# Memory attention's scores as three products of rounded halves

## The reference, cut to what matters

```python
def memory_cross_attention(h, mem_n, w_cq, w_ck, w_cv, w_co):
    q = (h @ w_cq).reshape(bsz, seqlen, 4, 256)
    k = (mem_n @ w_ck).reshape(bsz, mlen, 4, 256)
    v = (mem_n @ w_cv).reshape(bsz, mlen, 4, 256)
    logits = jnp.einsum('bqhd,bkhd->bhqk', q, k,
                        preferred_element_type=jnp.float32) * (256 ** -0.5)
    p = jax.nn.softmax(logits, axis=-1)
    o = jnp.einsum('bhqk,bkhd->bqhd', p.astype(v.dtype), v).reshape(bsz, seqlen, 1024)
    return o @ w_co
```

## Time and profile before

| what | value |
|---|---|
| median of 3 runs | 2120.2 us (2120.08 to 2120.25) |
| the profiled execution's own time | 2120.16 us |
| its span, first to last instruction | 2118.3 us |
| TensorE, matmul records, busy | 2108.1 us (100%) |
| TensorE, weight loads, busy | 1741.2 us (82%) |
| VectorE busy | 826.1 us (39%) |
| ScalarE busy | 808.3 us (38%) |
| GpSimd busy | 1120.8 us (53%) |
| granted TensorE clock | 1.000 of full speed |

### The profile page before, as it was taken

The page is one execution under the profiler, slowest core; times in us unless marked ns, Lnnn a source line. Parts: engine busy times, 40 slices in busy tenths (PEclk is TensorE's granted clock), DMA queues, the critical chain, the costliest instruction groups (busy, mean ns, idle before and its releaser), DMA issues.

```text
span 2118.3 us, 29185 instructions
## 1 busy us (share of the span) xinstructions
PE 2108.1 (100%) x10122; PEld 1741.2 (82%) x10122; DVE 826.1 (39%) x1486; ACT 808.3 (38%) x1364; POOL 1120.8 (53%) x1493
## 2 busy tenths in 40 slices
PE   9999999999999999999999999999999999999999
PEld 7888888878888778877888888887787898888898
DVE  5222211762941766143322221208753374013234
ACT  5222222325833656323322232325654353122234
POOL 6555555673344338725655555554454476555554
PEclk9999999999999999999999999999999999999999
DMA  6322333223322213412332223232222223332222
GB/s 212 122 99 99 99 100 110 85 96 102 116 89 90 73 58 123 156 40 90 99 99 93 95 99 110 100 97 73 80 80 80 90 90 105 103 100 99 99 90 80
DMA packets 61344, 207.71 MB, mean 98 GB/s; under 512 B 6616, under 2 KB 8088, under 8 KB 61256
## 3 DMA queue, kind: packets, MB, share of 16 engines
q1 hardware_dynamic: 55216, 195.84, 27.9%
q10 hardware_dynamic: 6040, 10.65, 1.6%
HBM read 204.31 MB, written 4.77 MB: 99 GB/s over the span
## 4 chain that ended last, share of the span: by engine, by line
PE 54%; issue 22%; POOL 21%; DVE 1%; ACT 1%; DMA 0%; POOLq 0%; SPq 0%; ACTq 0%; DVEq 0%
POOL w_lo L469 21%; PE bank L522 15%; PE bank L524 15%; PE bank L523 15%; PE bank L684 1%; PE bank L686 1%; PE bank L685 1%; PE bank L950 1%; PE bank L925 1%; PE bank L848 1%; PE bank L937 0%; DMA x<-xT 0%; PE bank L854 0%; PE bank L747 0%; PE bank L852 0%
## 5 line engine op out<-in xcount | busy, mean ns | idle before, releaser
L469 POOL TENSOR_TENSOR w_lo<-w_raw,w_hi 128x256 fp32r<-128x256 f32 x1448 | 1087.2, 783 | 926.7 <-ACT w_hi L1305 926.6
L522 PE MATMUL bank<-gx_hi,w_hi 128*128 128x512 f32 (+1 forms) x1768 | 674.4, 381 | 1.4 <-DVE gx_lo L2461 1.0
L524 PE MATMUL bank<-gx_hi,w_lo 128*128 128x512 f32 (+1 forms) x1768 | 668.1, 378 | 0.0
L523 PE MATMUL bank<-gx_lo,w_hi 128*128 128x512 f32 (+1 forms) x1768 | 667.6, 378 | 0.0
L1305 ACT CAST w_hi<-w_raw 128x1024 fp32r<-128x1024 f32 x364 | 378.5, 1045 | 346.1 <-PE bank L524 285.0
L522 PEld LDWEIGHTS bank<-gx_hi,w_hi 128*128 128x128 f32 x1768 | 332.7, 188 | 64.6 <-issue 2.3
L524 PEld LDWEIGHTS bank<-gx_hi,w_lo 128*128 128x128 f32 x1768 | 332.6, 188 | 62.4
L523 PEld LDWEIGHTS bank<-gx_lo,w_hi 128*128 128x128 f32 x1768 | 332.8, 188 | 60.5 <-issue 0.2
L522 PE MATMUL bank<-ff_hi,w_hi 128*128 128x512 f32 x352 | 136.9, 389 | 0.0
L523 PE MATMUL bank<-ff_lo,w_hi 128*128 128x512 f32 x352 | 136.9, 389 | 0.0
L524 PE MATMUL bank<-ff_hi,w_lo 128*128 128x512 f32 x352 | 136.9, 389 | 0.0
(11 more groups left out here) (361 smaller groups left out, 2703.5 us busy)
## 6 DMA issues: line engine op xcount, KB each, us to landing
w_raw<-wstream SPq DMA_DIRECT2D x364, 512.0 KB, 3.5
bias_spread<-bias_rows ACTq DMA_DIRECT2D x1, 2560.0 KB
square<-cum_rows ACTq DMA_DIRECT2D x8, 256.0 KB, 3.7
rfin_row<-cum_rows ACTq DMA_DIRECT2D x8, 256.0 KB, 3.2
outT<-ple_o SPq DMA_DIRECT2D x8, 256.0 KB, 2.0
x<-xT SPq DMA_DIRECT2D x3, 512.0 KB, 8.1
square<-bias_spread ACTq DMA_DIRECT2D x4, 256.0 KB, 2.6
rfin_row<-bias_spread ACTq DMA_DIRECT2D x4, 256.0 KB, 2.7
```

Of the source, the lines that this page charges most:

```text
L469: ins = nc.gpsimd.tensor_tensor(w_lo[:, s, part], w_raw[:, s, part], w_hi[:, s, part].bitcast(F32), ALU.subtract)
L522: nc.tensor.matmul(dst, hi, rhs[0], start=first, stop=False)
L523: nc.tensor.matmul(dst, hi, rhs[1], start=False, stop=False)
L524: return nc.tensor.matmul(dst, lo, rhs[0], start=False, stop=last)
```

## The change

The keys `kx_T` are rounded by ScalarE into `kx_hi` (in `round_k`, between the weight units of `cv`), and VectorE makes the rest `kx_lo`, in place of `kx_T`, when the last unit of `cv` is done. Each query chunk is rounded by ScalarE into `qx_hi` (`round_q`), and VectorE makes `qx_lo` in place of `qx_T` (`low_q`). `x_score` is then six matmuls of rounded operands instead of two in full fp32, and a head's first score waits for `score_lo`. `scale_q` moves from the end of VectorE's odd iterations to their start, and `low_q` takes its place at the end. Two semaphores of memsets are replaced by VectorE's own chain.

```diff
+        kx_hi = at("kx_hi", 16, [DC, ML], F32R)
+        kx_lo = at("kx_lo", 0, [DC, ML], F32R)
+        qx_hi = at("qx_hi", 24, [DC, S], F32R)
+        qx_lo = at("qx_lo", 48, [DC, S], F32R)
...
                 if i == 0:
-                    pe.wait_ge(tile_free, TILE0["cq"] + 2 * hd + 2)
-                for e in range(2):
-                    mm = nc.tensor.matmul(bank[2 + n % 2][:, 0:ML], qx_T[:, 2 * hd + e, i * P:(i + 1) * P],
-                                          kx_T[:, 2 * hd + e, :], start=(e == 0), stop=(e == 1))
+                    pe.wait_ge(sem("score_lo"), DC + 2 * hd + 2)
+                dst = bank[2 + n % 2][:, 0:ML]
+                for c in (2 * hd, 2 * hd + 1):
+                    qh, ql = (q[:, c, i * P:(i + 1) * P] for q in (qx_hi, qx_lo))
+                    nc.tensor.matmul(dst, qh, kx_hi[:, c, :], start=(c == 2 * hd), stop=False)
+                    nc.tensor.matmul(dst, qh, kx_lo[:, c, :], start=False, stop=False)
+                    mm = nc.tensor.matmul(dst, ql, kx_hi[:, c, :], start=False, stop=(c == 2 * hd + 1))
                 mm.then_inc(sem("x_score"), 1)
...
+            def round_k(c):
+                act.wait_ge(tile_free, TILE0["ck"] + c + 1)
+                nc.scalar.copy(kx_hi[:, c, :], kx_T[:, c, :]).then_inc(sem("score_hi"), 1)
             for g in range(2):
-                token_evac("cv", g, vx, m_rstd, MT, ACT.Copy, (sem("m_col"), 1), banks=CV_BANKS[g])
+                token_evac("cv", g, vx, m_rstd, MT, ACT.Copy, (sem("m_col"), 1), between=round_k, banks=CV_BANKS[g])
             ahead("cq", 0, 4, 0)
             norm("n_cross")
             ahead("cq", 0, 4, 1)
             ahead("cq", 0, 4, 2)
+
+            def round_q(c):
+                act.wait_ge(tile_free, TILE0["cq"] + c + 1)
+                nc.scalar.copy(qx_hi[:, c, :], qx_T[:, c, :]).then_inc(sem("score_hi"), 1)
+            round_q(0)
+            round_q(1)
             for n in range(XH * TT + 4):
+                if n % 2 == 1 and n < 12:
+                    round_q(2 + n // 2)
...
-            nc.vector.memset(conv_in[:, 0:3], 0.0).then_inc(sem("conv_pad"), 1)
-            dve.wait_ge(sem("conv_pad"), 1)
+            link(nc.vector.memset(conv_in[:, 0:3], 0.0))
...
             scaled_tiles("ck", kx_T, 8, row=m_row, banks=CK_BANKS)
+            dve.wait_ge(unit_done, UNIT0["cq"])
+            for c in range(DC):
+                dve.wait_ge(sem("score_hi"), c + 1)
+                nc.vector.tensor_tensor(kx_lo[:, c, :], kx_T[:, c, :], kx_hi[:, c, :].bitcast(F32), ALU.subtract)\
+                  .then_inc(sem("score_lo"), 1)
             norm("n_cross")
...
+            def low_q(c):
+                dve.wait_ge(sem("score_hi"), DC + c + 1)
+                nc.vector.tensor_tensor(qx_lo[:, c, :], qx_T[:, c, :], qx_hi[:, c, :].bitcast(F32), ALU.subtract)\
+                  .then_inc(sem("score_lo"), 1)
             scale_q(0)
             scale_q(1)
+            low_q(0)
+            low_q(1)
             for n in range(XH * TT + 5):
+                if n % 2 == 1 and n < 12:
+                    scale_q(2 + n // 2)
...
                 if n % 2 == 1 and n < 12:
-                    scale_q(2 + n // 2)
+                    low_q(2 + n // 2)
...
-            nc.vector.memset(cprod[:, 0:2], 0.0).then_inc(sem("cprod_pad"), 1)
+            link(nc.vector.memset(cprod[:, 0:2], 0.0))
```

## The result

| what | before | after |
|---|---|---|
| median of 11 runs each, side by side | 2120.33 us (2120.08 to 2122.21) | 2125.78 us (2124.98 to 2127.52) |
| ratio after to before | | 1.0024, interval 1.0016 to 1.0033 |
| profiled execution's span | 2118.3 us | 2124.7 us |
| granted TensorE clock | 1.000 | 0.998 |

The change costs 5.5 us, slower by more than the 0.2% that was called measurable. The forecast was 2119.5, its range 2117.5 to 2121.5: wrong in size and in sign.

A forecast was written before the change was run, and what follows sets the result against it. TensorE was taken as the bound, its matmul records covering 2108.1 of 2118.3 us. Scores -2.6, keys 0, first query chunks +1.9 and other heads 0 gave -0.7 us from 2120.16: 2119.5, range 2117.5 to 2121.5.

The forecast's parts named there:

- term 2: Key rests after `cv`: eight subtractions, 7.0 us in all, covered, so 0 us; uncovered 0 to 1 us.
- term 3: First two query chunks: rounding and subtraction delay the first score, a stall of 1.9 us (0.8 to 2.0).
- Term 1: Scores: six matmuls take 0.71 us a block instead of 0.87, gaining 2.6 us over 16 (2.2 to 3.5).
- Term 4: Other heads and the two memsets: `low_q` has 1.3 us of cover or more, so 0 us.
- D: `score_lo` late at every head: three more stalls of 1.9 us, 2125.2 us; chance 0.04.
- E: Six score matmuls bound by their weight loads, 1.13 us instead of 0.71: 6.7 us more, 2126.2; chance 0.03.
- Rival C: VectorE late for the row of `n_cross`, or GpSimd for the second `cq` tile: 0.6 to 1 us, 2120.3; chance 0.06.
- The lock: Port shared by VectorE and GpSimd: exclusive blocking would make a pair 1.14 us; the sum used the trace's 0.88.

The follow-up runs named there:

- the dead additions at 849.5 and 860.4: The kernel before plus one VectorE addition of two SBUF tiles whose result nothing reads, started at 849.49 or 860.39 us: 2124.27 and 2124.36 us.
- the copy: The kernel before plus one VectorE copy from SBUF to SBUF whose result nothing reads, when `cv` is done: 2122.50 us.
- the addition at 854.7: The kernel before plus one VectorE addition of two SBUF tiles whose result nothing reads, when unit 2 of `cv` is done: 2122.76 us.
- the memset: The changed kernel with a VectorE memset of 0.17 us in front of the first `kx_lo`: 2124.64 us.
- one dead addition's run: The kernel before plus one VectorE addition of two SBUF tiles whose result nothing reads, when `cv` is done, ahead of `n_cross`: 2120.61 us.

## Why the prediction was wrong

**The failed step is term 2, "The keys, nothing".** It priced eight subtractions at the pair's pitch of 0.88 us and wrote them off against a cover of 1.5 us. The pitch was right for a VectorE that gets its turn: with a short break in GpSimd's run the eight were over at 878.10. But here the first one got no turn for 10.7 us, and the row of `n_cross` came 4.3 us late. The rows that I took the pitch from are from a stretch in which VectorE comes every microsecond or two; the place of the change is one in which it had met GpSimd for the last time near 833 us and GpSimd had worked through 37 us since the earlier trace rows. That difference stood in the rows and went unused: `cv` has VectorE at 0.00. The profiled execution lies 7.0 us above the forecast: 4.3 are the late row, 1.6 the half clock behind it, 1.6 the second stretch, 0.3 what the scores gave less there, and term 3 takes back 0.8.

**What it hung on.** With the norm first: -5.8 us. With a pause in GpSimd: -6.7. Those are the same cure twice, for both take away the late row (4.3 us) and the clock's fall behind it (1.6); the norm first trades the first score's stall for one of 1.7 us at a bank.

**The clock, not in the prediction at all.** After a gap of 4.56 us TensorE was granted 0.50 (1.2 GHz of 2.4) for 3.4 us, worth 1.6 us over the 24 products (all gaps here are counted from start to start). After gaps at the row of 2.34 and 2.37 us it fell to 0.50 too (the dead additions at 849.5 and 860.4); after gaps of 2.19 and 2.37 (the copy, and the addition at 854.7) it stayed at 1.00, and their times are 2122.50 and 2122.76 against 2124.27 and 2124.36: the fall is worth 1.5 to 1.9 us there too. After 3.9 us behind the memset it stayed at 1.00 there and fell at 1363.5. The windows at 884 to 886 us of the additions from 849.5 and 854.7, a fence for each kernel (busy, then the granted clock):

```profile
884.00:886.00 2.00, 2.00 (x6) 0.50 0.39 154
```

```profile
884.00:886.00 2.00, 2.00 (x10) 1.00 0.44 174
```

So the gap's length alone doesn't settle the fall; what else does stays open, as does the cause of the second stretch near 1366.

**Term 1, the scores: right.** 0.15 us saved a block, forecast 0.16; the six matmuls stand 0.12 us apart, forecast 0.118. With the stalls out of the way the whole change gave 2.6 us, the forecast's sum for it.

**Term 3, the first score: mis-sized.** The stall was 1.1 us where I took 1.9 of 0.8 to 2.0. The two `qx_lo` took 1.95 us together, 0.81 and 1.21, where I had put 2.38: only the second met a whole GpSimd piece. ScalarE's two casts stand 0.53 us apart, not 0.62, since each starts before the record ahead of it ends, and so does the first of them behind the weight cast. The first score starts 0.05 us behind `qx_lo`, not up to 0.3. The row's delay has no part in it; with the row in time (the pause) the stall was the same. The mechanism was right: moving the weight cast removed it.

**Term 4, the other heads, and the memsets: right**, no gap at any. Rivals D and E did not happen; that the measured 2125.8 lies near D's 2125.2 and E's 2126.2 is chance. Rival C named the right place, VectorE late for the row, but priced it at 0.6 to 1 us with turns of one to one; it was 4.3 us.

**The lock.** I weighed the Trainium skill (SBUF — State Buffer, Who interferes with whom), by which the second instruction blocks until the first is through, against 0.88 us a pair, and let the pair decide. Neither gives 10.7 us: blocking for one GpSimd piece is 0.70 us. But the same rule of the Trainium skill, that an operation with two SBUF inputs contends with GpSimd and may block fully, stood nearer to what happened than a sum of average turns.

What stays open: why the memset's and one dead addition's run let VectorE in at a change of weight unit (878.9 and 879.1) and the others didn't, where between 7.2 and 10.0 us the limit lies and whether it is the same in every execution, and by what mechanism VectorE is passed over: no run shows that.

## What to carry to other kernels

Before placing an SBUF-to-SBUF operation on VectorE, look at how long GpSimd has worked without a break or a turn at that point: a contended duration read from one place holds only for places with runs as short as that one's. Put what TensorE waits for ahead of such an operation in VectorE's order, not behind it, and give the operation an input in PSUM where there is one, or place it behind the run's end. And price a new TensorE gap of a size seen here, 2.3 us and up, at its length plus what the clock may take behind it, here 1.5 to 1.9 us.

## What the runs showed of the hardware

- A VectorE operation of 128x256 fp32 that needs 0.41 us can last 32.8 us: beside a GpSimd run 10.0 us old or older at its start, with turns given neither at GpSimd's pieces every 0.70 us nor at eleven changes of weight unit. At an age of up to 7.2 us it waited for one piece at most (0.84 and 0.82 us).
- A break of 0.67 us in GpSimd's run, or contention kept up every 3 us, restores the turns (0.96 us each, 0.88 apart).
- A copy from SBUF to SBUF with one input is shut out too (10.59 us); an addition with one input in PSUM and one in SBUF isn't (0.42 us).
- The granted clock fell to 0.50 for 3.4 us behind gaps of 2.34, 2.37 and 4.56 to 4.60 us and not behind gaps of 1.97, 2.19, another of 2.37, and 3.9 us; at the gap of 9.1 us it was at 0.50 for 10.2 us.
